# Norms of keys kept compact, g matrices turned and inputs stacked ahead of the kernel taps, scores on four quadrants with masks applied later, and products of constants in TensorE's waits

## The chip, the cores and the metric

One core of one Trainium2 chip runs the whole kernel. The metric is the device time of one execution in microseconds (us), as the median of several runs. Smaller is better.

## What is computed

One decoder layer for 256 tokens of width 1024, all in float32 (gathers and biases in bfloat16 parts). Cut to what matters:

```python
h = rms_norm(x, norm_mix_g)
proj = h @ w_in                                   # 1024 x 2048
y_s5 = s5_mixer(proj[:, :512], ...)               # diagonal complex state space, gelu, glu
y_rw = rwkv7_mixer(h, r, k, v, ...)               # 8 heads of 64
    # kk = k*k_k / |k*k_k| per head; decay; a; g;
    # state = state*w + (state . -kk)(kk*a) + v k;  y = state . r
x = x + concat(y_s5, y_rw) @ w_out
h = rms_norm(x, norm_moe_g)
logits = h @ router_w + router_b                  # top 4 of 32 experts
for e in experts: act = swiglu(h @ w_gate[e] + b, h @ w_up[e] + b); y = act @ w_down[e] + b
x = x + moe;  x = x + sigmoid(rms_norm(x) @ ple_w_gate) * (p @ ple_w_proj);  return rms_norm(x)
```

## The kernel before, in words

All tiles lie in one arena of 47 units of 4 KB per partition (`un(i)`); eight PSUM banks are shared by all stages. Each engine has its program written out by hand, and semaphores (`s[...]`) join them. Three blocks follow one another, with a barrier of all engines between them: the mixers (`layer`, from L276), the router (L1243) and the expert loop (L1379), then a tail (L1549).

**Mixers.** TensorE sums squares (L851 on), then `project(n)` makes 256 columns of the input projection at a time, in `order`, and ScalarE copies each out (`copy_proj`, L395). The low-rank paths follow (`lora_out`, L408, L410). For the S5 mixer VectorE builds products of constants (`products`, L615 to L620), ScalarE pads them into `gpad` (L427) and `opad` (L448), and TensorE makes the `kernel_taps`, turns the 32 `gpad` matrices (`turn_g`, L894; copies at L468), lays out the inputs (`stack_u`; copies at L471) and multiplies (`into`). VectorE takes the phase off (`phase_off`, L635 to L640), scans and puts it back (`phase_on`, L650 to L657). For the RWKV mixer, sums of squares of the keys per head come out as full 128x512 tiles (`head_sums`), with a root on ScalarE (L441) and maximum and reciprocal over 1024 columns on VectorE (L705, L706). The time is cut into 4 chunks of 64; a unit is a chunk of a pair of heads, 16 in all. `pair` issues two 64x64 products, head h on rows and columns h. Five scores of 16 units each come first, masked by VectorE as it copies them from PSUM (L748 to L752). A triangular inverse in 5 levels follows: products `W` (MO by X), a copy by ScalarE (L477), products by Y, an addition by VectorE (L781) and its transpose (L737). In between TensorE turns three arrays (`turn`; copies at L481) and makes the S5 output (`s5_out`; VectorE L661). Then four chunks in turn (ScalarE L486, L492, L496; VectorE L817, L818), with the glu (L501) and parts of the output projection between, and a normalisation (L799 to L811) before the rest of the projection.

GpSimd splits the expert biases into bfloat16 parts (L340 to L344) once their DMAs have landed. SyncE issues the DMAs in a written order, with waits between; a weight slot cannot be filled before the tiles in the same units have been read.

**Router.** Logits, top 4, gates, ranks (VectorE), then the gates are transposed (L1351) and four products of 32 rows with `exp_b_down` start the output accumulation in four banks (L1221).

**Experts.** Each of 32 experts has six chunks of 2 MB (gate 2, up 2, down 2), in a ring of eight slots. Chunks 0, 4 and 5 of expert 0 are issued in the mixers (L304), chunk 1 near their end (L325), chunks 2, 3 and 7 at the start of the router block, chunk 6 at the start of the expert block (L1384), and each later one when TensorE has used the chunk that lies eight before it (L1389). TensorE gathers the tokens (needs the one-hot of L1431), multiplies chunk by chunk, scatters. L1221 and L239 are the `mm` helpers, so most matmuls have one of these lines.

## Time and profile before

| | |
|---|---|
| median of 3 runs | 1209.95 us (1209.51 to 1210.59) |
| profiled execution, its own time | 1203.81 us |
| its span, first to last instruction | 1202.0 us |
| TensorE busy, VectorE, ScalarE, GpSimd | 90%, 30%, 15%, 1% |
| moved by DMA | 430.28 MB, 358 GB/s over the span |
| mean granted TensorE clock | 0.991 |

The busy shares are averages over stages with different limits: the mixers take about the first 220 us, the router 20 us, the experts the rest. A float32 matmul stands in the trace as two records, each with its weight load. Times from the span's start are used below.

### The profile page before, as it was taken

The numbers are of one execution on the slowest core, as the hardware profiler recorded it, in microseconds if no ns is written. First come the engines' busy times: TensorE is split into PE (matmuls) and PEld (weight loads), VectorE is DVE, ScalarE is ACT, GpSimd is POOL, SyncE is SP. The second block draws the span as 40 slices with busy tenths as digits, with TensorE's granted clock in tenths as the row PEclk, the third lists the DMA queues.
The fourth block names the chain that finished last, engine by engine and source line by source line (L and its number), as shares of the span: only waits on it lengthen the run. The fifth ranks groups of instructions, "written<-read, shape, count | busy, mean of one in ns | idle before, by whom it ended". The sixth has DMA issues, their size and how long they took to land. (4 is left out here: it accounts for less than half of the span.)

```text
span 1202.0 us, 18872 instructions
## 1 busy us (share of the span) xinstructions
PE 1076.2 (90%) x8132; PEld 492.5 (41%) x8132; DVE 365.5 (30%) x739; ACT 176.3 (15%) x288; POOL 17.5 (1%) x18
## 2 busy tenths in 40 slices
PE   6989998899999988888888888888888888888896
PEld 5779884443334333333333333333333333333342
DVE  5997925522222111111222111111111221211122
ACT  5580231400000000000000000000000000000023
POOL 0000005000000000000000000000000000000000
PEclk9989999899999999999999999999999999999999
DMA  9301184589999999999999999999999999999970
GB/s 324 125 2 37 43 328 142 211 359 426 428 428 430 428 429 428 427 428 429 429 429 430 428 429 428 428 428 430 429 429 428 429 428 428 427 430 428 430 289 35
DMA packets 44531, 430.28 MB, mean 358 GB/s; under 512 B 4912, under 2 KB 15536, under 8 KB 19920
## 3 DMA queue, kind: packets, MB, share of 16 engines
q1 hardware_dynamic: 44304, 429.24, 85.5%
q8 instruction: 28, 0.46, 0.2%
q0 software_dynamic: 192, 0.52, 0.1%
q14 instruction: 7, 0.06, 0.0%
HBM read 428.70 MB, written 1.05 MB: 358 GB/s over the span
## 5 line engine op out<-in xcount | busy, mean ns | idle before, releaser
L1221 PE MATMUL bank<-arena 128*64 128x512 f32 (+5 forms) x5136 | 847.3, 467 | 91.0 <-DMA arena<-in_exp_w_up 58.3
L1221 PEld LDWEIGHTS bank<-arena 128*64 128x64 f32 (+4 forms) x5136 | 307.8, 128 | 607.0 <-issue 446.2
L239 PE MATMUL bank<-arena 64*64 64x64 f32 (+7 forms) x2048 | 161.6, 264 | 15.4 <-ACT arena L362 8.5
L239 PEld LDWEIGHTS bank<-arena 64*64 64x64 f32 (+3 forms) x2048 | 129.3, 144 | 45.7 <-issue 26.3
L1410 ACT ACTIVATE arena<-arena 128x512 f32<-128x512 f32 x32 | 20.1, 630 | 520.2 <-DVE arena L1458 520.2
L1463 DVE TENSOR_SCALAR arena<-bank 128x512 f32<-128x512 f32 x32 | 22.1, 691 | 227.7 <-PE bank L1221 227.7
L1473 DVE COPY arena<-bank 128x512 f32<-128x512 f32 x32 | 22.1, 691 | 202.8 <-PE bank L1221 202.8
L1458 DVE TENSOR_SCALAR arena<-bank 128x512 f32<-128x512 f32 x32 | 22.1, 691 | 194.0 <-PE bank L1221 194.0
L1413 ACT ACTIVATE arena<-bank 128x256 f32<-128x256 f32 x32 | 12.3, 383 | 326.2 <-PE bank L1517 326.2
L1434 DVE TENSOR_TENSOR arena<-bank,par 128x512 f32<-128x512 f32 x33 | 22.8, 691 | 77.9 <-PE bank L1221 77.9
L1466 DVE SCALAR_TENSOR_TENSOR arena<-arena 128x512 f32<-128x512 f32 x32 | 33.7, 1052 | 1.1
L1461 DVE TENSOR_TENSOR arena<-arena 128x512 f32<-128x512 f32 x32 | 22.1, 692 | 24.5 <-ACT arena L1410 24.5
L1415 ACT ACTIVATE arena<-bank 128x512 f32<-128x512 f32 x32 | 19.1, 597 | 1.7
L1521 PE MATMUL bank<-con,arena 128*128 128x128 f32 x128 | 19.2, 273 | 0.0
L1446 DVE TENSOR_SCALAR arena<-con,arena 128x128 f32<-128x128 f32 x64 | 19.1, 340 | 0.1
L1431 DVE TENSOR_SCALAR arena<-con,arena 128x64 bf16<-128x64 f32 x66 | 13.8, 251 | 14.3 <-PEq L1243 7.5
L1517 PEld LDWEIGHTS bank<-con,arena 128*128 128x128 f32 x64 | 6.5, 141 | 24.3 <-issue 24.3
L1521 PEld LDWEIGHTS bank<-con,arena 128*128 128x128 f32 x128 | 15.0, 140 | 0.0
L239 PE MATMUL bank<-arena,con 128*32 128x64 f32 (+1 forms) x144 | 11.4, 322 | 3.6 <-ACT arena L506 1.4
L1517 PE MATMUL bank<-con,arena 128*128 128x128 f32 x64 | 14.1, 301 | 0.0
L1410 ACT ACT_TABLE_LOAD x8 | 10.3, 1283 | 7.8 <-PEq L1243 7.7
L352 ACT ACTIVATE arena<-par 128x2048 f32<-128x2048 f32 (+1 forms) x7 | 10.3, 1533 | 0.0
(275 smaller groups left out, 406.7 us busy)
## 6 DMA issues: line engine op xcount, KB each, us to landing
arena<-in_exp_w_gate SPq DMA_DIRECT2D x64, 2048.0 KB, 32.2
arena<-in_exp_w_down SPq DMA_DIRECT2D x64, 2048.0 KB, 35.4
arena<-in_exp_w_up SPq DMA_DIRECT2D x64, 2048.0 KB, 35.3
arena<-in_w_in SPq DMA_DIRECT2D x8, 1024.0 KB, 12.9
arena<-in_w_out SPq DMA_DIRECT2D x4, 1024.0 KB, 6.3
...
```

Of the source, the lines that this page charges most:

```text
L239: return nc.tensor.matmul(out, lhsT, rhs, start=start, stop=stop, skip_group_check=True)
L1221: return nc.tensor.matmul(out, lhsT, rhs, start=start, stop=stop, skip_group_check=True)
L1410: nc.scalar.activation(sg, gt, ACT.Sigmoid, scale=1.702).then_inc(s["sig_ready"], 1)
L1415: nc.scalar.activation(actT[:, :, :, :], GATE[:, :].rearrange("p (k h s) -> p k h s", h=2, k=4), ACT.Copy).then_inc(s["actT_ready"], 1)
L1434: tt(xg[:, :, :], GAT[:, :].rearrange("p (k s) -> p k s", k=KD), prm("g_moe_run")[:, :, None].to_broadcast([P, KD, SLOTS]), ALU.mult).then ...
L1458: ts(gt, GATE[:, :], 7.0, None, ALU.min).then_inc(s["gt_ready"], 1)
L1461: tt(sg, sg, gt, ALU.mult).then_inc(s["swish_ready"], 1)
L1463: ts(up, UP[:, :], 7.0, -7.0, ALU.min, ALU.max).then_inc(s["up_read"], 1)
L1466: stt(by_run(gt), plain(up), 1.0, plain(sg), ALU.add, ALU.mult).then_inc(s["act_ready"], 1)
L1473: V.tensor_copy(y, YB[:, :]).then_inc(s["y_ready"], 1)
L1517: last = nc.tensor.transpose(YB[:, t * P:(t + 1) * P], pg[:, t, :], ident)
L1521: last = nc.tensor.transpose(GATE[:, k * P:(k + 1) * P], gt[:, k * P:(k + 1) * P], ident)
```

## The change

- Start: 20 products of ones with ones on TensorE before the squares are summed.
- Keys' norms: the squares are the stationary operand and 2 columns of head sums the moving one, so that 16 numbers per token tile come out; root, maximum and reciprocal run over 128x16; 16 products with the identity spread them again; VectorE multiplies out of PSUM.
- Order: ScalarE pads g after the low-rank outputs, copies the first g matrix of each (`gfirst`) for the taps; `turn_g` is in two halves around `project(4)` and the norms; `stack_u` comes ahead of `kernel_taps`. GpSimd does three memsets that ScalarE (clear of units 2, 3) and VectorE (EL) did.
- Token shift of k and v: ScalarE multiplies by 1 - mu, VectorE adds the shifted rest in 4 instructions instead of 6. ScalarE also scales rk.
- Scores: units 8 to 15 of each score go to the other half of the columns (`cross=True`), interleaved with units 0 to 7; ScalarE copies Mx, RB and RK unmasked, VectorE masks RB and RK in levels 3 and 4. The scans of `phase_on(1)` run ahead of the scores. Head sums of rk move into level 0, `s5_out(3)` into level 4, between its two sets of products. `turn` is in four quadrants too. Chunks 2 and 3 have crossed halves and waits on `first_half`.
- Router: router bias loaded in the mixers; 4 products of constants; gates laid out in four row groups, `exp_b_down` loaded four times, in four DMAs, so that the four bias products use four row groups; 5 products of constants before the first gather. In the expert loop two semaphore waits of VectorE become one.

```diff
+        rbias = bb[:, 0, 0:E]
+        head_pair = head_ones[:, 0:P:CH]
+        norms, rest_mu = u0[:, 0:4 * TT * 2], u0[:, 32:32 + 2 * FT].rearrange("p (m f) -> p m f", f=FT)
...
+                a, o = slice(h * CH, (h + 1) * CH), slice((h ^ cross) * CH, (h ^ cross) * CH + CH)
+                last = mm(out[o], lhsT[a], rhs[a], start, stop)
...
+                sp.dma_start(rbias, io["router_b"].to_broadcast([P, E])).then_inc(p_in, 16)
...
-                sp.dma_start(bias_down, io["exp_b_down"]).then_inc(bias_in, 16)
+                for r in range(4):
+                    hf = r % 2
+                    sp.dma_start(bias_down[r * E:(r + 1) * E, :], io["exp_b_down"][:, hf * 512:(hf + 1) * 512]).then_inc(bias_in, 16)
...
+                pool.wait_ge(s["proj_done"], at_place[0])
+                nc.gpsimd.memset(EL, 1.0).then_inc(s["pool_set"], 1)
+                pool.wait_ge(s["pool_set"], 1)
+                nc.gpsimd.memset(EL[:, :, 0::CH], 0.0).then_inc(s["pool_set"], 1)
+                pool.wait_ge(s["proj_done"], at_place[1])
+                nc.gpsimd.memset(un(2, 2), 0.0).then_inc(s["pool_set"], 1)
...
+                act.wait_ge(s["proj_copied"], at_place[5])
+                rest_of_shift(0, raw["k"], kx, "shift_rest")
...
                 lora_out(0)
...
                 lora_out(1)
                 act.wait_ge(s["kk_ready"], 1)
                 A(kksq[:, :, :], kkn[:, :, :], ACT.Square).then_inc(s["kk_squared"], 1)
+                act.wait_ge(s["pads_clear"], 7)
+                for m in range(2):
+                    act.wait_ge(s["built"], m + 1)
+                    for g in range(2):
+                        a, o = half(g)
+                        A(gpad[m][a, :, :, o].rearrange("p j n c -> p n j c"), gprod[m][a], ACT.Copy).then_inc(s["padded"], 1)
                 copy_proj(2)
                 lora_out(2)
+                act.wait_ge(s["kk_summed"], 1)
+                A(norms, banks[6][:, 0:4 * TT * 2], ACT.Sqrt).then_inc(s["kk_norm"], 1)
+                for m in range(2):
+                    for g in range(2):
+                        a, o = half(g)
+                        A(gfirst[a, m, :, o], gprod[m][a, 0], ACT.Copy).then_inc(s["padded"], 1)
...
-                act.wait_ge(s["kk_summed"], 1)
-                for b in range(2):
-                    m = A(kb[:, 2 * b:2 * b + 2, :], banks[4 + b].rearrange("p (f t) -> p f t", t=T), ACT.Sqrt)
-                m.then_inc(s["kk_root"], 1)
+                for n in range(4):
+                    copy_g(n)
...
-                clear(2, 2)
+                for n in range(4, 8):
+                    copy_g(n)
...
-                A(mag_run[:, :, 1:NK], s5p[:, 15, :][:, :, None].to_broadcast([P, NJ, NK - 1]), ACT.Copy).then_inc(s["mag_ready"], 1)
-                copy_proj(4)
                 copy_proj(5)
-                act.wait_ge(s["pads_clear"], 7)
+                for b in range(2):
+                    act.wait_ge(s["stacked"], b + 1)
+                    A(ustack[:, 8 * b:8 * b + 8, :], banks[2 + b].rearrange("p (j k) -> p j k", k=NK), ACT.Copy).then_inc(s["ustack_ready"], 1)
+                act.wait_ge(s["pool_set"], 3)
                 act.wait_ge(s["taps_done"], 1)
...
+                A(mag_run[:, :, 1:NK], s5p[:, 15, :][:, :, None].to_broadcast([P, NJ, NK - 1]), ACT.Copy).then_inc(s["mag_ready"], 1)
                 copy_proj(6)
+                act.wait_ge(s["scaled"], 3)
+                for i in range(FT):
+                    last = A(rk[:, i, :], rk[:, i, :], ACT.Copy, scale=prm("r_k")[:, i:i + 1])
+                last.then_inc(s["rk_ready"], 1)
                 copy_proj(7)
+                act.wait_ge(s["proj_copied"], 8)
+                rest_of_shift(1, raw["v"], vv, "shift_rest")
+                for m, dst in ((1, Mx), (3, RB), (4, RK)):
+                    for b in range(2):
+                        act.wait_ge(s["scores_done"], 2 * m + b + 1)
+                        A(dst[:, 8 * b:8 * b + 8, :], banks[SCORE_BANK[m] + b].rearrange("p (u t) -> p u t", t=CH), ACT.Copy).then_inc(s["scores_moved"], 1)
...
-                dve.wait_ge(s["proj_done"], at_place[0])
-                link(V.memset(EL, 1.0))
-                link(V.memset(EL[:, :, 0::CH], 0.0))
+                dve.wait_ge(s["pool_set"], 2)
...
+                dve.wait_ge(s["kk_norm"], 1)
+                link(ts(norms, norms, 1e-12, None, ALU.max))
+                V.reciprocal(norms, norms).then_inc(s["kk_norm"], 1)
...
-                dve.wait_ge(s["kk_root"], 1)
-                link(ts(kb, kb, 1e-12, None, ALU.max))
-                link(V.reciprocal(kb, kb))
-                link(tt(kkn, kkn, kb, ALU.mult))
+                dve.wait_ge(s["kk_summed"], 2)
+                for b in range(2):
+                    d = kkn[:, 2 * b:2 * b + 2, :]
+                    last = tt(d, d, banks[6 + b].rearrange("p (f t) -> p f t", t=T), ALU.mult)
+                last.then_inc(s["kk_norm"], 1)
+                dve.wait_ge(s["kk_norm"], 3)
...
+                phase_scan(0)
                 phase_on(0)
                 phase_off(1)
+                phase_scan(1)
...
+                for b in range(2):
+                    dve.wait_ge(s["scores_done"], b + 1)
+                    d = X[:, 8 * b:8 * b + 8, :]
+                    link(tt(d, banks[SCORE_BANK[0] + b].rearrange("p (u t) -> p u t", t=CH), col(C_SU1), ALU.mult))
+                    link(tt(d, d, eye, ALU.add))
+                    turn_x(b).then_inc(s["scores_copied"], 1)
+                for b in range(2):
+                    dve.wait_ge(s["scores_moved"], b + 1)
+                    level_mask(0, b)
+                for b in range(2):
+                    dve.wait_ge(s["scores_done"], 4 + b + 1)
+                    tt(KA[:, 8 * b:8 * b + 8, :], banks[SCORE_BANK[2] + b].rearrange("p (u t) -> p u t", t=CH), col(C_SU), ALU.mult).then_inc(s["scores_copied"], 1)
+
+                phase_on(1)
...
+                    if lev >= LEVELS - 2:
+                        dst = (RB, RK)[lev - LEVELS + 2]
+                        dve.wait_ge(s["scores_moved"], 6)
+                        for b in range(2):
+                            d = dst[:, 8 * b:8 * b + 8, :]
+                            tt(d, d, col(C_UI), ALU.mult).then_inc(s["scores_masked"], 1)
...
+                for _ in range(20):
+                    mm(banks[0][:, 0:P], ones_early, ones_early, True, True)
...
-                head_sums(kksq, 4).then_inc(s["kk_summed"], 1)
+                for n in range(4 * TT):
+                    tok = slice(n // FT * P, (n // FT + 1) * P)
+                    last = mm(banks[6][:, 2 * n:2 * n + 2], kksq[:, n % FT, tok], head_pair, True, True)
+                last.then_inc(s["kk_summed"], 1)
+                turn_g(0)
                 project(4)
+                pe.wait_ge(s["kk_norm"], 2)
+                for n in range(4 * TT):
+                    tile, f = n // FT, n % FT
+                    for h in range(2):
+                        last = mm(banks[6 + f // 2][h * CH:(h + 1) * CH, (f % 2) * T + tile * P:(f % 2) * T + (tile + 1) * P],
+                                  norms[:, 2 * n + h:2 * n + h + 1].to_broadcast([P, CH]), ident, True, True)
+                last.then_inc(s["kk_summed"], 1)
+                turn_g(1)
                 project(5)
+                stack_u()
+                pe.wait_ge(s["kk_norm"], 3)
                 kernel_taps()
-                turn_g()
-                stack_u()
...
+                    bank = SCORE_BANK[m]
+                    for u in range(8):
+                        o = slice(u * CH, (u + 1) * CH)
+                        ins = pair(banks[bank][:, o], fm(l, u), fm(r, u))
+                        if u == 7:
+                            ins.then_inc(s["scores_done"], 1)
+                        last = pair(banks[bank + 1][:, o], fm(l, u + 8), fm(r, u + 8), cross=True)
+                    last.then_inc(s["scores_done"], 1)
...
+                    if lev == 0:
+                        pe.wait_ge(s["rk_ready"], 1)
+                        pe.wait_ge(s["scores_copied"], 4)
+                        head_sums(rk, 0).then_inc(s["rk_summed"], 1)
+                    if lev == LEVELS - 1:
+                        s5_out(FT - 1)
...
-                pe.wait_ge(s["xy_ready"], 2 * LEVELS)
                 pe.wait_ge(s["turned"], 6)
                 pe.wait_ge(s["bonus_ready"], 1)
+                pe.wait_ge(s["scores_masked"], 4)
...
                     if c:
                         pe.wait_ge(s["u0_ready"], c)
                     for i, o in enumerate(tiles):
-                        pair(banks[0][:, o], KA[:, c * FT + i, :], Vs[:, c * FT + i, :], i == 0, False)
+                        last = pair(banks[0][:, o], KA[:, c * FT + i, :], Vs[:, c * FT + i, :], i == 0, False)
+                    if cross:
+                        last.then_inc(s["first_half"], 1)
                     if c:
                         pe.wait_ge(s["y_copied"], c)
                     for i, o in enumerate(tiles):
-                        pair(banks[5][:, o], Vs[:, c * FT + i, :], RK[:, c * FT + i, :], i == 0, False)
+                        last = pair(banks[5][:, o], Vs[:, c * FT + i, :], RK[:, c * FT + i, :], i == 0, False, cross)
+                    if cross:
+                        last.then_inc(s["first_half"], 1)
                     if c:
                         pe.wait_ge(s["state_ready"], c)
+                    if cross:
+                        pe.wait_ge(s["first_half"], 3 * c - 4)
                     for i, o in enumerate(tiles):
-                        last = pair(banks[0][:, o], fm(at, c * FT + i), state[:, o], False, True)
+                        last = pair(banks[0][:, o], fm(at, c * FT + i), state[:, o], False, True, cross)
...
+            for _ in range(4):
+                mm(banks[7][:, 0:P], ident, ident, True, True)
             pe.wait_ge(s["gates_ready"], 1)
-            for tile in range(TT):
-                last = nc.tensor.transpose(banks[5][0:E, tile * P:(tile + 1) * P], gates[:, tile, :], ident)
+            rows = [slice(n * E, (n + 1) * E) for n in range(4)]
+            for n in range(4):
+                last = mm(banks[5][rows[n], 0:P], gates[:, n // 2, :], ident, True, True)
             last.then_inc(s["gates_turned"], 1)
             pe.wait_ge(s["gatesT_ready"], 1)
+            pe.wait_ge(s["ple_copied"], EARLY)
             for n in range(4):
-                if n < EARLY:
-                    pe.wait_ge(s["ple_copied"], n + 1)
-                mm(banks[n][:, :], gatesT[:, n // 2 * P:(n // 2 + 1) * P], bias_down[:, n % 2 * HF:(n % 2 + 1) * HF], True, False)
+                mm(banks[n][:, :], gatesT[rows[n], :], bias_down[rows[n], :], True, False)
...
+            for _ in range(5):
+                mm(YB[:, 0:P], ident, ident, True, True)
```

## Rows read from the trace of the kernel before

**Rows 1.** The page, part 2: GB/s moved in 40 equal slices of the span.

```profile
GB/s 324 125 2 37 43 328 142 211 359 426 428 428 430 428 429 428 427 428 429 429 429 430 428 429 428 428 428 430 429 429 428 429 428 428 427 430 428 430 289 35
```

**Rows 2.** Waits of TensorE, 250 to 1160 us: total us, times, longest.

```profile
PE bank L1221 <- DMA arena<-in_exp_w_up: 58.3, 52, 1.2
```

**Rows 3.** Busy by window: PE, PEld, DVE, ACT, POOL; PEclk; DMA share; GB/s.

```profile
80.00:82.00 2.00, 1.05 (x5) 1.05 (x6) 1.97 (x2) 1.98 (x5) 0.00 (x0) 0.53 0.00 0
...
238.00:240.00 2.00, 1.39 (x2) 0.00 (x0) 0.00 (x0) 0.00 (x0) 0.00 (x0) 0.50 0.62 262
240.00:242.00 2.00, 0.91 (x18) 0.91 (x19) 0.42 (x2) 1.28 (x1) 0.00 (x0) 0.50 0.15 33
...
248.00:250.00 2.00, 2.00 (x12) 0.70 (x10) 0.00 (x0) 0.00 (x0) 0.00 (x0) 1.00 0.41 74
```

**Rows 4.** Timeline at the hand-over: start, us, engine, line; idle before in brackets.

```profile
232.94 6.46 PE L1221 MATMUL bank<-arena 32*128 32x512 f32 x8 [0.46 <-ACT arena L1273]
...
241.09 2.74 PE L1221 MATMUL bank<-arena 128*128 128x64 bf16 x48 [1.70 <-DVE arena L1431]
...
248.62 3.68 SPq L1389 DMA_DIRECT2D arena<-in_exp_w_up  x2
```

**Rows 5.** Timeline of the start, and of project(3) for comparison.

```profile
8.52 5.33 PE L239 MATMUL bank<-arena 128*128 128x256 f32 x16 [8.52 <-ACT arena L362]
...
13.89 0.47 ACT L369 ACTIVATE arena<-bank,par 128x256 f32<-128x256 f32 x1 [1.43 <-PE bank L239]
...
46.95 7.17 PE L239 MATMUL bank<-arena 128*128 128x256 f32 x32
```

**Rows 6.** Timeline of ScalarE and TensorE, 47 to 85 us.

```profile
47.78 4.29 ACT L427 ACTIVATE arena<-arena 64x1024 f32<-64x1024 f32 x4
...
68.70 1.91 ACT L352 ACTIVATE arena<-par 128x2048 f32<-128x2048 f32 x1
...
76.95 1.06 ACT L395 ACTIVATE arena<-bank 128x512 f32<-128x512 f32 x2
...
80.95 3.68 PE L894 MATMUL bank<-con,arena 128*128 128x128 f32 x16 [4.56 <-ACT arena L468]
```

**Rows 7.** Timeline of VectorE, 84 to 111 us.

```profile
84.41 1.20 DVE L667 TENSOR_TENSOR arena<-arena 128x1020 f32<-128x1020 f32 x1
...
92.21 0.69 DVE L635 TENSOR_TENSOR arena<-bank,arena 128x512 f32<-128x512 f32 x1 [2.01 <-PE bank L239]
...
96.12 2.34 DVE L650 TENSOR_TENSOR_SCAN arena<-arena 128x512 f32<-128x512 f32 x2
...
110.74 0.69 DVE L748 TENSOR_TENSOR arena<-bank,con 128x512 f32<-128x512 f32 x1 [4.09 <-PE bank L239]
```

**Rows 8.** Timeline of small products: taps, five scores, one turned array.

```profile
72.46 1.82 PEld L239 LDWEIGHTS bank<-arena 128*32 128x32 f32 x128 [0.33 <-issue]
...
109.54 9.41 PEld L239 LDWEIGHTS bank<-arena 64*64 64x64 f32 x320 [0.33 <-issue]
...
141.21 2.03 PE L239 MATMUL bank<-con,arena 64*64 64x64 f32 x64
```

**Rows 9.** Timeline of the levels and of the first chunk.

```profile
119.84 1.96 PE L239 MATMUL bank<-arena,con 128*128 128x512 f32 x4 [0.75 <-DVE arena L752]
...
121.73 6.74 PE L239 MATMUL bank<-arena 64*64 64x64 f32 x209
...
138.63 0.60 ACT L477 ACTIVATE arena<-bank 128x512 f32<-128x512 f32 x1 [2.85 <-PE bank L239]
...
146.73 0.60 ACT L477 ACTIVATE arena<-bank 128x512 f32<-128x512 f32 x1 [2.84 <-PE bank L239]
...
158.38 1.15 PE L239 MATMUL bank<-arena 64*64 64x64 f32 x32 [0.79 <-DVE arena L781]
```

**Rows 10.** Timeline of VectorE and GpSimd at the normalisation.

```profile
198.81 3.64 DVE L808 TENSOR_SCALAR arena<-arena,par 128x128 f32<-128x128 f32 x4
...
200.83 1.03 POOL L344 CAST arena<-arena 32x1024 bf16<-32x1024 f32 x1
```

207 lines of the change are left out of this document (97 added, 110 removed).

## The prediction, made before the change was run

> **What bounds the kernel now.** I read the DMA rates first, then who waits for whom, then the hand-over from router to experts, then the mixers. From the tenth slice on the DMA moves 425 to 430 GB/s without a break [rows 1]: the expert weights. TensorE waits for them, 52 times for the up chunks alone [rows 2], so the expert loop ends when its stream ends, and a faster TensorE or VectorE in it buys nothing. The stream cannot start early: the slots lie in units that the mixers and the router use. A first load after the barriers goes out late, and the continuous part begins only when TensorE has used chunk 0, at 248.62 [rows 4]. Whatever brings that moment forward moves the end by as much. Around it the DMA is short of full rate: 262, 33 and 74 GB/s against 428 in three windows of 2 us [rows 3], which is 0.8 + 1.85 + 1.65 = 4.3 us of stream, and the windows between are short too. That bounds what the hand-over can give: its gain ends once the queue no longer runs dry, somewhere over 4.3 us. What comes before the router block counts in full.
>
> **Start.** TensorE sums squares in 5.33 us for 16 records of 256 columns; later 32 such records take 7.17, 0.224 each [rows 5]. So 16 would be 3.6 us, and the first few ran at half speed, 1.2 GHz by their duration. The 20 new products (40 records of 128 columns, 0.11 us at full and 0.22 at half speed, half of the 0.224) start at about 1.1 us. Some 3.5 us at half speed, then full, end them near 7.3, ahead of the squares. The sums then end 1.7 us earlier. The root waited 1.43 us for them [rows 5], the rest being its table load, so the gain is 1.4. Bounds: if they stay at half speed to the end they end near 10.1 and delay the sums by 1.6, which gives back all but a little; if the first weights land just then, 0. I take 1.4.
>
> **ScalarE to copy_proj(5).** VectorE cannot shift r before this copy, which ended at 78.0 [rows 6]. ScalarE is busy all the way from 46 us, so I count its work. Out: the clear 1.9; the mag copy 1.1, now behind; the root of 1024 columns 1.1 for one of 16 columns 0.2. In: eight copies of turned g at 0.53 (a 128x512 copy, half of 1.06), 4.3; four copies of gfirst, between 0.2 and 1.07 each (a quarter of the 4.29), the elements being a quarter, so 0.35: 1.4. The root also waits for the norm sums behind `lora_out(2)`; the table load covers most of their 2 us, 1.1 is left. The padding of g only changes its place. With 1.4 from the start: 78.0 - 1.9 - 1.1 - 0.9 + 4.3 + 1.4 + 1.1 - 1.4 = 79.5. The shift of r began at 84.41 [rows 7], since VectorE was held by 1024-column reciprocals and maxima that now vanish; it begins at 79.7.
>
> **VectorE to the scores.** Shift, rk and rt take until 92.21 - 2.01 = 90.2, that is 5.8 us, giving 85.5; the 2.01 us wait for `into` falls away, since TensorE has turned g and stacked u by then: its stall of 4.56 us [rows 6] and the half clock behind it (0.53 granted, 1.2 GHz) [rows 3] go. From 92.21 to 110.74 - 4.09 = 106.65 VectorE works on phases for 14.4 us: 99.9. The second scan with two products, 2.34 + 2 x 0.69 = 3.7, is now before the scores: 103.6. TensorE is ready for them at about 102: 7.5 of its 109.54, the same stall and slow stretch less some 2 us of products that spread the norms, in place of nothing. So VectorE is late next. Masking X begins at 103.6 in place of 110.74.
>
> **Scores.** X takes two times 0.69 + 0.69 + 0.7, till 107.8. TensorE's RB score waits for that (its banks), then ScalarE copies RB, 2 x 0.6, and level 0 starts. On two quadrants 320 records take 9.41 us, 29.4 ns each; the taps, on four column groups, 1.82 us for 128, 14.2 ns each at the same mean of 64 columns [rows 8]. I take four quadrants at that rate: a score 0.95 us in place of 1.9. Level 0 starts at 107.9 + 0.95 + 1.3 = 110.2 in place of 121.73 [rows 9]: 11.5 earlier. The masks of RB and RK, the copy of Mx, the rk scaling (ScalarE, under `project(7)`) leave this chain.
>
> The Trainium skill ("TensorE: Matmul & The Clock Gate", section "Wait — 56ns, not 53.3ns?") says that matmuls never start closer together than about 25 ns. The 14.2 ns of [rows 8] disagree with it. By that rule the scores would gain 0.3 us each and turns 0.3 us, and the sum would come out 3 us higher.
>
> **Levels.** They are bound by TensorE, a level each 146.73 - 138.63 = 8.1 us [rows 9]. Head sums of rk move in, 1.96 [rows 9]. Each of three `turn` falls from 2.03 [rows 8] to 1.0, but behind the third nothing else stands now and the RB mask (2 x 0.65) delays VectorE's addition, so it gives 0.4. `s5_out(3)` only changes place. The first chunk saves 0.79 of waiting for X, yet its glu waits for the gelu as before, so I take 0. Together 1.96 - 1.0 - 1.0 - 0.4 = -0.4: the first chunk starts 11.9 earlier.
>
> **Chunks and normalisation.** Four waits on `first_half` let TensorE drain; never less than 0, at most one record's 0.224 us each: +0.4, about the middle. GpSimd's split starts when the bias DMAs have landed; three more DMAs, and the weights' loads nearer by, make that 1 to 2 us later against the loop. It ran till 201.9, and beside it VectorE took 3.64 us for four 128x128 operations [rows 10]. Two more operations now fall beside it: +0.6 (0 to 1.5). So the router block starts 10.9 earlier. Memsets on GpSimd lie under VectorE's wait before r; uncovered they would cost 1 us.
>
> **Hand-over.** The four bias products take 6.46 us, at half clock [rows 3, 4]. In four row groups they take one's time, 0.9 at full and 1.7 at half clock: -5.5 (-4.7). The barrier follows at once, since the other engines have nothing behind these products. The five products start about when VectorE starts its one-hot, 0.5 us before the gather: 1.1 to 2.2 us of work, +0.6 to +1.7. The gather took 2.74 at 0.50 granted clock [rows 3, 4]; at full clock half: 0 to -1.4. Together -3.0 to -6.3, capped by the idle DMA. I take -5.0, nearer the upper end since 4 products keep TensorE busy ahead of the drop.
>
> **Sum.** 11.9 - 0.4 - 0.6 + 5.0 = 15.9 us. Against the profiled 1203.81 that is 1187.9; the median lies 6.1 above that execution, and so 1194.1. The merged wait in the expert loop is worth 0, under the DMA; uncovered it is some 0.1 us per expert.
>
> **Rivals.**
> *More quadrants bring nothing.* For it: no row shows all four at once with different rows and columns. Against: [rows 8]. Price: 1.0 at RB, 2.4 at the turns, 2.6 at the bias products in series at full clock: 1200.1. Chance 0.10.
> *The clock falls among the scores.* TensorE idles from about 104.8 to 107.9 for X. It fell to 0.53 behind the 4.56 us stall [rows 3, 6]; this gap is shorter. Some 3 us of work at half speed would be added: 1197.1. Chance 0.20. The Trainium skill ("TensorE: Matmul & The Clock Gate", section "What's actually happening") calls the half clock the default to which an idle TensorE returns; with that the trace agrees.
> *ScalarE or the norms are later.* ScalarE's chain has no slack left, and a late item (turned g, norms, u) stops TensorE and then VectorE. At 4 us: 1198.1. Chance 0.16.
> *Slower.* The clock falls as above and the levels do not lift it: the 32-row products ran at half clock till they ended without lifting it [rows 3, 4], and the levels' tiles are of 64. Price: the 36 us from level 0 to the chunks, doubled: 1230. It decides once more than 16 us of TensorE-bound work runs at half clock. Head sums on all rows speak against it. Chance 0.04.
> *Nothing arrives.* The stream would be held by something not tied to the mixers: 1210. [rows 2, 4] speak against. Chance 0.05.
>
> **Numbers.** The forecast has 0.45: 1194.1. Upward, quadrants, clock and late ScalarE reach 1200 together with a flat start and a hand-over at -3; downward the hand-over's full 6.3 and no cost at the normalisation give 1191.8, and some ends I can't see. I take 1189.5 to 1202. A measurement of this kernel tells 0.2% (2.4 us) from no change. Faster 0.91, same 0.05, slower 0.04.
>
> **What would show it.** Root near 12.5; the r shift near 80; X near 103.6; level 0 near 110; first chunk near 146.5; bias products in 1 to 2 us; first refill about 16 us before 248.6, and the tail as far ahead. Wrong: a granted clock of 0.5 between 105 and 180, scores at 29 ns per record, or a router block that starts over 14 or under 7 us earlier.

## The result, and the profile after

The changed kernel takes 1200.73 us, the median of 9 runs (1198.24 to 1209.95); the kernel before, beside it on the same chip, takes 1209.51, the median of 9 (1204.73 to 1210.59). The ratio is 0.9947, with a 95% interval from 0.9924 to 0.997. So it is faster, by about 6.4 us. The forecast of 1194.1 was 6.6 us too low, though the time lies in the range. The runs of each kernel scatter about as widely as the two differ (5.9 us those of the kernel before, 11.7 those of the changed one), which will matter below.

The two profiled executions differ by less: 1200.06 against 1203.81 us, span 1198.3 against 1202.0. They are what the sum was made on: it said -15.9, and -3.7 came. That the median missed by only 6.6 is luck: the forecast put it 6.1 above the profiled execution, as in the kernel before, and it lies 0.7 above.

The timeline of the changed kernel (start, us, engine, line; idle before and its releaser in brackets), from several stretches, of all five engines:

```profile
12.49 0.47 ACT L383 ACTIVATE arena<-bank,par 128x256 f32<-128x256 f32 x1
16.36 29.93 PE L243 MATMUL bank<-arena 128*128 128x256 f32 x144 [4.19 <-DMA arena<-in_w_in]
48.14 7.17 PE L243 MATMUL bank<-arena 128*128 128x256 f32 x32
...
106.74 0.69 DVE L803 TENSOR_TENSOR arena<-bank,con 128x512 f32<-128x512 f32 x1 [0.39 <-PE bank L243]
111.10 0.33 PE L243 MATMUL bank<-arena 64*64 64x64 f32 x4 [2.60 <-DVE arena L798]
112.36 5.60 PE L243 MATMUL bank<-arena 64*64 64x64 f32 x188 [0.93 <-issue]
127.20 2.37 PE L243 MATMUL bank<-arena 64*64 64x64 f32 x74 [1.29 <-issue]
...
186.46 1.04 POOL L354 CAST arena<-arena 128x1024 bf16<-128x1024 f32 x1 [129.28 <-DMA arena<-in_exp_b_down]
194.70 6.45 DVE L865 TENSOR_SCALAR arena<-arena,par 128x128 f32<-128x128 f32 x4
203.49 13.06 PE L243 MATMUL bank<-arena 128*128 128x512 f32 x24 [4.76 <-DVE arena L868]
...
223.78 0.82 SPq L1344 DMA_DIRECT2D arena<-in_exp_w_up  x2
234.97 1.14 PE L1315 MATMUL bank<-arena 32*128 32x512 f32 x8 [0.40 <-ACT arena L1368]
238.55 1.56 PE L1315 MATMUL bank<-arena 128*128 128x64 bf16 x48
244.90 3.68 SPq L1486 DMA_DIRECT2D arena<-in_exp_w_up  x2
```

And the windows of the changed kernel, with the columns of [rows 3]: busy PE, PEld, DVE, ACT, POOL; granted clock; DMA share; GB/s.

```profile
16.00:18.00 2.00, 1.65 (x6) 1.46 (x7) 2.00 (x6) 2.00 (x2) 0.00 (x0) 0.85 1.11 353
18.00:20.00 2.00, 2.00 (x6) 1.55 (x6) 1.97 (x2) 1.98 (x3) 0.00 (x0) 0.50 1.05 380
...
106.00:108.00 2.00, 2.00 (x152) 2.00 (x148) 1.58 (x3) 1.97 (x6) 0.00 (x0) 1.00 0.57 147
...
112.00:114.00 2.00, 1.64 (x81) 1.64 (x84) 2.00 (x5) 0.29 (x1) 0.00 (x0) 0.74 0.03 8
114.00:116.00 2.00, 1.88 (x65) 1.70 (x60) 1.91 (x3) 1.38 (x4) 0.00 (x0) 0.50 0.00 0
...
202.00:204.00 2.00, 0.51 (x1) 0.50 (x2) 1.97 (x3) 0.00 (x0) 0.16 (x1) 0.50 0.00 0
...
238.00:240.00 2.00, 2.00 (x55) 1.98 (x53) 0.15 (x1) 0.58 (x1) 0.00 (x0) 1.00 0.94 401
```

The kernel before at the same places (its matmuls are L239): the first projections, the gap in its levels, GpSimd's split, the output products, and the router block's first load.

```profile
16.88 28.21 PE L239 MATMUL bank<-arena 128*128 128x256 f32 x144 [3.03 <-DVE arena L556]
129.56 3.71 PE L239 MATMUL bank<-arena 64*64 64x64 f32 x119 [1.09 <-issue]
186.18 1.04 POOL L340 CAST arena<-arena 128x1024 bf16<-128x1024 f32 x1 [182.65 <-DMA arena<-in_exp_b_down]
203.96 10.57 PE L239 MATMUL bank<-arena 128*128 128x512 f32 x24 [1.16 <-DVE arena L811]
222.15 0.90 SPq L1249 DMA_DIRECT2D arena<-in_exp_w_up  x2
```

Read from top to bottom. The root starts at 12.49 as forecast, but TensorE then waits 4.19 us for the first weights, its clock falls to half, and project(3) starts at 48.14, later than before [rows 5]. X is masked at 106.74, 4.0 us earlier than in [rows 7]; behind the scores TensorE waits 2.60 us for those masks, then 0.93 for nothing that the profile shows, and the clock is at half again. In the levels it stands still again, 1.29 us and then 0.60. The first chunk starts at 154.26, 4.1 earlier than [rows 9]. All of that is lost at the normalisation: four 128x128 operations take 6.45 us, TensorE waits 4.76 for them, its clock falls, and the router block's first load goes out at 223.78, 1.6 us later than before (222.15). The hand-over (from the router block's first load to the first refill, the load that starts the unbroken stream) then gives 5.35: from that load to the first refill 21.1 us in place of 26.5, with the bias products in 1.14 us and the gather in 1.56 at full clock, where [rows 4] have 6.46 and 2.74. The refill at 244.90 is 3.7 earlier than [rows 4], as the end is.

So there are four places to explain: the front, the scores and levels, the normalisation, and the hand-over that came out right.

### The profile page after: what moved, and what is told of

The parts are those of the page before. It is cut to its first block and busy times, and to the rows that moved or that the text cites. A ratio compares the mean times of both kernels' runs of the same rounds, so it can differ in the third digit from the quotient of the medians.

```text
span 1198.3 us, 19087 instructions
## 1 busy us (share of the span) xinstructions
PE 1076.2 (90%) x8240; PEld 494.3 (41%) x8240; DVE 357.3 (30%) x730; ACT 183.5 (15%) x309; POOL 20.4 (2%) x21
## 5 line engine op out<-in xcount | busy, mean ns | idle before, releaser
L243 PE MATMUL bank<-arena 64*64 64x64 f32 (+8 forms) x2088 | 169.7, 272 | 16.8 <-DVE arena L868 4.8
L243 PEld LDWEIGHTS bank<-arena 64*64 64x64 f32 (+3 forms) x2088 | 134.7, 152 | 48.5 <-issue 25.2
L1512 ACT ACTIVATE arena<-bank 128x512 f32<-128x512 f32 x32 | 19.1, 598 | 1.7
L243 PE MATMUL bank<-arena,con 128*32 128x64 f32 (+1 forms) x140 | 8.4, 255 | 1.9 <-ACT arena L547 1.4
L409 ACT ACTIVATE arena<-bank 128x512 f32<-128x512 f32 x8 | 5.8, 721 | 25.0 <-PE bank L243 25.0
```

The source lines that it names most:

```text
L243: return nc.tensor.matmul(out, lhsT, rhs, start=start, stop=stop, skip_group_check=True)
L1512: nc.scalar.activation(actT[:, :, :, :], GATE[:, :].rearrange("p (k h s) -> p k h s", h=2, k=4), ACT.Copy).then_inc(s["actT_ready"], 1)
```

## The experiments

The kernel before ran beside each set on the same chip. Times below are those of the profiled execution (span) unless a median is named. The experiments are called e1 to e17, after the labels of their expectations; those at the front (e1, e6), e3, e4, e9, e10 and e11 are single runs.

### The front

The first test takes the 20 warm-up products out, the second keeps them and puts 12 more behind the sums of squares.

```diff
-                for _ in range(20):
-                    mm(banks[0][:, 0:P], ones_early, ones_early, True, True)
```

> The changed kernel without the 20 products ahead of the sums of squares; all else as changed. Theory W: the products gain nothing, because project(0) waits for its weights (16.36 us in the changed kernel, 16.88 before), and they lengthen TensorE's idle stretch ahead of it from 3.0 to 4.2 us, in which the granted clock falls to 0.50. Without them project(0) starts at 16.9, its records take 0.22 us each, no window from 16 to 24 shows a clock under 1, project(3) starts at 46.9 to 47.2 instead of 48.14, the shift of r (VectorE) at 80.7 to 81.0 instead of 81.98, and the first chunk 1.1 us earlier. Rival: the slow stretch has another cause (DMA, ScalarE's clear of the ninth unit); then project(3) stays at 48.1 or comes later, by the 0.5 us of the later start.

```diff
                 last.then_inc(s["rms_summed"], 1)
+                for _ in range(12):
+                    mm(banks[0][:, 0:P], ones_early, ones_early, True, True)
```

> The changed kernel with 12 more of the warm-up products, behind the sums of squares, where TensorE waits 4.19 us for the first weights. Nothing is left out. Theory (the early sums only lengthen the wait for the weights, and behind it the clock falls to half for 4 us of project(0)): project(0) still starts at 16.4 to 16.7, since the weights land then, but runs at full clock and takes 28.2 us in place of 29.93, project(3) starts at 46.4 to 46.8 in place of 48.14, the shift of r 1 to 1.7 us before 81.98, and the end comes 1 to 2 us before 1198.3. Rival (the load of the weights is what is slower, 13.6 against 12.9 us): project(0) takes 29.5 to 30 again, and nothing moves by more than 0.4.

TensorE's timeline without the warm-up products:

```profile
8.46 5.65 PE L243 MATMUL bank<-arena 128*128 128x256 f32 x16 [8.46 <-ACT arena L376]
17.14 28.21 PE L243 MATMUL bank<-arena 128*128 128x256 f32 x144 [3.03 <-DVE arena L601]
47.21 7.17 PE L243 MATMUL bank<-arena 128*128 128x256 f32 x32
```

TensorE's timeline with 12 more of them, and two windows of that kernel below it:

```profile
16.59 7.61 PE L243 MATMUL bank<-arena 128*128 128x256 f32 x34 [1.55 <-DMA arena<-in_w_in]
...
46.69 7.17 PE L243 MATMUL bank<-arena 128*128 128x256 f32 x32
```

```profile
16.00:18.00 2.00, 1.41 (x7) 1.26 (x8) 2.00 (x6) 2.00 (x2) 0.00 (x0) 1.00 1.11 351
18.00:20.00 2.00, 2.00 (x11) 1.77 (x10) 1.97 (x2) 1.98 (x3) 0.00 (x0) 1.00 1.05 380
```

Without the products (e1) the first weights are used 0.8 us later (17.14 against 16.36), and project(3) still starts 0.9 us earlier, because the first projections take 28.21 us in place of 29.93. With the bridge (e6) the clock stays at 1.00, project(3) starts at 46.69 and the shift of r at 80.53, 1.45 us before the changed kernel; the end came at 1196.1. The load isn't slower, as the rival had it: the weights land at 16.3 to 16.6 in every kernel with the warm-up. So the warm-up does what was forecast for the sums (3.72 us for the 16 records where it is read alone), and the time it saves is waited away in front of the weights, long enough for the clock to fall. Behind waits of 4.02 to 4.24 us it fell in all 12 traces that have the warm-up and no bridge, behind 1.55 and 1.56 in the two with the bridge it stayed up. A wait of 3.03 us decides nothing by itself: the clock stayed up behind it in the kernel before, in e1 and in e16, and fell in e8, which also leaves out the warm-up (further down):

```profile
18.20 29.62 PE L243 MATMUL bank<-arena 128*128 128x256 f32 x144 [3.03 <-DVE arena L601]
```

```profile
18.00:20.00 2.00, 1.80 (x4) 1.51 (x5) 2.00 (x7) 2.00 (x2) 0.00 (x0) 0.50 1.06 380
```

There project(3) starts at 49.67, later than in the changed kernel. So to leave the warm-up out is no sure cure; to fill the wait was one in both traces that have it.

### The normalisation

First the split of the biases was held back until VectorE's normalisation is over, then its loads were moved ahead of those of w_out and the slots, so that the split is done before it.

```diff
                 pool.wait_ge(s["bonus_ready"], 1)
+                pool.wait_ge(s["mix_rw_ready"], 2)
...
-                        act.wait_ge(s["bias_split"], 10)
+                        act.wait_ge(s["bias_split"], 5)
```

> The changed kernel with GpSimd's split of the expert biases held back until both token tiles are normalised (it then runs beside the last output products); ScalarE's wait before it overwrites the first bias tile asks for the 5 steps that read that tile, and no more for all 10. Theory G: in the changed kernel the split falls beside VectorE's first normalisation, because the chunks end 4 us earlier while the bias DMAs land no earlier; both slow down (four 128x128 operations in 6.45 us, 3.64 before, 1.11 alone), TensorE then waits 4.76 us and its clock falls to 0.50 for some 6 us. Held back, the four operations take 1.1 us, TensorE's wait before the output products is under 1 us, its clock stays at 1, and the router block starts 7 to 9 us earlier, at 215 to 217 instead of 223.8; some of it is given back where the split meets VectorE's residual. The end comes 5 to 9 us earlier. Rival: VectorE's slowness has another cause than GpSimd; then the router block stays at 223 to 224.

Its VectorE, first at the normalisation, then at the residual:

```profile
194.45 1.12 DVE L866 TENSOR_SCALAR arena<-arena,par 128x128 f32<-128x128 f32 x4
...
208.19 3.23 DVE L896 TENSOR_SCALAR arena<-arena,small 128x1024 f32<-128x1024 f32 x1
```

```diff
-                sp.wait_ge(s["s5_out_done"], 4)
-                for c in (1, 2):
-                    sp.dma_start(wout[c][:, :, :], wo[c]).then_inc(wout_in, 16)
...
                 sp.wait_ge(s["scaled"], 4)
                 sp.wait_ge(s["phase_on"], 2)
...
+                sp.wait_ge(s["s5_out_done"], 4)
+                for c in (1, 2):
+                    sp.dma_start(wout[c][:, :, :], wo[c]).then_inc(wout_in, 16)
...
```

> The changed kernel, but the loads of the expert biases are issued before the loads of wout and the slots (their own waits kept), and the load of wproj behind them. Nothing is left out. GpSimd's split, which now runs from 186.5 to 202.2 beside VectorE's normalisation, should then run beside the chunk loop and be done before the last y copy. Theory N (the normalisation lost about 5 us because the split still ran beside it, so that four 128x128 operations take 6.45 us in place of 1.1 and TensorE's clock falls): the row of four operations falls to 1.1 to 1.5, TensorE's wait of 4.76 us is gone, the router block's first load goes out 3 to 5 us before 223.8, and the span falls by 3 to 4.5, so about 1194 to 1195.5 against 1198.3. Rival M (contention only moves, as it did when the split was held back): the chunk loop's VectorE operations are slowed, the last y copy comes 3 us or more later than 187.7 and the router block starts within 1 us of 223.8.

(The lines left out take the loads of the slots, pT, the router's bias and wproj along, behind those of the expert biases.) Its GpSimd, VectorE and TensorE:

```profile
147.42 1.04 POOL L354 CAST arena<-arena 128x1024 bf16<-128x1024 f32 x1 [90.03 <-ACT arena L522]
...
162.44 1.11 POOL L358 CAST arena<-arena 32x1024 bf16<-32x1024 f32 x1
...
191.10 17.33 PE L243 MATMUL bank<-arena 128*128 128x512 f32 x40
193.73 1.11 DVE L865 TENSOR_SCALAR arena<-arena,par 128x128 f32<-128x128 f32 x4
```

Held back (e2), the split lets the four operations run in 1.12 us, but meets the next ones: a 128x1024 scaling takes 3.23 us where it takes 1.26 in the changed kernel, and the router block's load goes out at 223.22, 0.6 us earlier. There is a second cost that I had overlooked: the barrier ahead of the router block waits for every engine, GpSimd too, and its split now ends at 222.4; TensorE stood idle for 8.1 us before 223.26, with its clock at half from 216.6. The contention was only moved (median 1202.37, ratio to before 0.9962, interval 0.9946 to 0.9979). Done early (e5), beside the chunk loop, it costs nothing there: the last y copy is at 187.13 (187.72 in the changed kernel), TensorE goes through its 40 records without a wait, and the load goes out at 215.65, 8.1 us earlier. The span is 1191.2, 7.1 less than the changed kernel's; I had expected 3 to 4.5. The profiled execution, 1192.96, is the fastest of 4; the others took 1195.04 to 1199.72. The median is 1196.97, the ratio to before 0.9906 (0.9886 to 0.9927), so by the ratios (0.9906 against 0.9947) the move is worth some 5 us.

The Trainium skill ("SBUF — State Buffer", section "SBUF: two separate sides") has VectorE and GpSimd share one pair of ports as an exclusive lock, held for a whole instruction, but for VectorE only where its operation runs in a mode with two ports or has two inputs in SBUF. The traces agree in form: the four operations took 1.6 us each beside GpSimd operations of 1.03 to 2.13 us and 0.28 alone, while the reciprocal, with one input, took 3.35 in both.

### The scores

Three tests (e3, e4, e7): the pairs back on two quadrants; 12 constant products in the gap before RB; and RB and RK in banks 2 and 3, so that the gap has no cause.

```diff
         def pair(out, lhsT, rhs, start=True, stop=True, cross=False):
+            cross = False
```

> The changed kernel with every crossed product put back on the straight halves (scores, turned arrays, chunks 2 and 3), so that only two quadrants of the array are used; order and everything else as changed. Theory Q: four quadrants give about 0.9 us per score and 0.7 us per turned array, but the first scores lie in a stretch in which VectorE is late, so that only the scores behind the masked X and the three turned arrays count. Level 0 starts 0.5 to 1.5 us later, each turned array takes 2.03 us instead of 1.33, and the first chunk starts 2 to 3.5 us later than 154.26. If TensorE's idle stretch ahead of the fourth score shrinks enough for the clock to stay at 1, 1 to 2 us of this come back. Rival: the four quadrants bring nothing; then the turned arrays take the same 1.3 us and the first chunk starts at 154 to 154.5.

Its windows behind the first three scores:

```profile
112.00:114.00 2.00, 1.60 (x50) 1.58 (x51) 2.00 (x5) 0.00 (x0) 0.00 (x0) 1.00 0.04 8
114.00:116.00 2.00, 2.00 (x76) 2.00 (x74) 1.97 (x5) 1.09 (x2) 0.00 (x0) 1.00 0.00 0
```

With two quadrants TensorE is busy for longer and waits only 0.63 us for X; its clock stays at 1.00 through scores and levels. In the changed kernel it runs 65 small records in the same window at half clock, here 76 at full. That is why the quadrants bought only 0.6 us at the first chunk (156.15 against 155.56 for its first copy) and 0.95 at the last y copy: 2 to 3.5 had been expected. Nor are these 0.6 earned in this stretch: the first score already starts 0.48 later than in the changed kernel (105.96 against 105.48).

```diff
                     if m == 3:
+                        for _ in range(12):
+                            mm(banks[2][:, 0:P], ident, ident, True, True)
                         pe.wait_ge(s["scores_copied"], 2)
```

> The changed kernel with 12 products of the identity with itself (a bank that nothing uses then) in TensorE's wait ahead of the fourth score. Theory C: TensorE stands idle for 2.6 us there after short work, the clock is granted at 0.50 to 0.74 from 112 to 116 us, and the fourth score, the fifth and the first products of level 0 run at half speed. With the 12 products (12 x 0.11 to 0.22 x 2 records, some 2.7 us) no window from 110 to 118 is under 1, the copies of RB end 1 us earlier than 114.8, level 0's first copy by ScalarE starts at 115 to 116 instead of 117.07, and the first chunk 1 to 2 us earlier than 154.26. Rival: the gap between the fourth score's first records and the rest (0.93 us, nothing seen to release it) is what costs, and it stays; then the gain is under 0.7 us.

```diff
-        SCORE_BANK = (4, 6, 0, 4, 6)
+        SCORE_BANK = (4, 6, 0, 2, 2)
...
-                    if m == 3:
-                        pe.wait_ge(s["scores_copied"], 2)
...
```

> The changed kernel, but the scores RB and RK go to banks 2 and 3 instead of 4 to 7, so that RB no longer waits for the masks of X, and level 0 no longer for the copy of RB. Nothing is left out. Theory C (the first three scores, in half the time, left TensorE idle for 2.6 us, its clock fell to half, and RB, RK and level 0 took back at half speed what the quadrants had gained): with that wait gone the granted clock stays at 1.00 from 104 to 125, RB is over by 110, RK by 112, the first W copy starts at 113 to 114 in place of 117.07, the first addition to X at 117 to 118 in place of 121.0, and the first chunk starts 3 to 3.7 us before 154.26. End: 2.5 to 3.7 us less than 1198.3. Rival V (VectorE with its masks and phases is the bound behind the scores): the W copy comes earlier, but the first addition to X no more than 1 us, and the end by under 1 us. Rival F (TensorE waits for its own instructions): gaps without a releaser of over 2 us appear between 105 and 125 and the W copy moves by under 2 us.

The edit moves other waits with the banks: RK waits for both copies of RB, level 0 for VectorE's masks of X, and `s5_out(0)` for the copies of RK.

TensorE's timeline with the 12 products:

```profile
112.54 3.89 PE L243 MATMUL bank<-con 128*128 128x128 f32 x19 [3.05 <-issue]
```

TensorE's timeline with the other banks:

```profile
113.91 1.15 PE L243 MATMUL bank<-arena 64*64 64x64 f32 x59 [3.75 <-issue]
116.24 5.38 PE L243 MATMUL bank<-arena 64*64 64x64 f32 x128 [1.18 <-ACT arena L514]
```

Both miss, and in the same way. The work that should have filled the gap didn't start: TensorE stood still for 3.05 and 3.75 us with every semaphore that it needs set, and then ran at half clock. In the second the first W copy came 2.9 us later than in the changed kernel (119.95), and the end at 1200.5 (median 1203.56; ratio to before 0.9972, 0.9952 to 0.9992); the first ended at 1198.3, as the changed kernel did. Of the 2.9 us, 1.55 came from ahead of the scores: the first began at 107.03 in place of 105.48, since the clock fell at 60.4 already, behind the small norm products of 128x2. It fell there, between 57.8 and 62.0, in six of the 17 traces (e7, e8, e11, e13, e16, e17), which no run explains. What was missing behind the scores were instructions. The DMA view of that stretch lists, beside 1 MB of w_out, the queue that brings them, three packets of 16 KB:

```profile
q1 hardware_dynamic: 272, 1.05, 18.7%
q8 instruction: 3, 0.05, 1.0%
```

The traces bear this out. In all 17 of this family the gaps without a releaser between taps and levels stand at the same places in the count of TensorE's matmul records from the start of the execution (600, 980 or 981, 1107, 1360, 1486, and so on, at distances that are multiples of some 127; no trace has all of them). They do so although the scores begin at record 784, in the kernels without warm-up at 744 and in those with the bridge at 808, so that 170 to 240 records of the stage are through when the first gap comes (in e11, where it is the next one, 323). And each ends 1.2 to 1.6 us after a packet of 16 KB of that queue is through: in the changed kernel the packet of 110.12 took 0.95 us, and TensorE goes on at 112.36; in e7 it is 111.60, 0.96 and 113.91. The gap lasts until the next packet has come.

That gave two theories, which the next pair tells apart by moving two w_out loads to the place of the other two.

```diff
-                sp.dma_start(wout[3][:, :, :], wo[3]).then_inc(wout_in, 16)
...
-                for c in (1, 2):
+                for c in (3, 0, 1, 2):
```

> The changed kernel with two of the four loads of w_out (1 MB each; they now go out at 105.6 and 120.3) moved behind the last s5_out product, at about 151, where the other two are. Nothing is left out. In the changed kernel TensorE stands still without a releaser for 0.93 us behind the first and 1.29 us behind the second of these loads. Theory B (its instructions are fetched by the same DMA engines, and wait behind the megabyte): both gaps shrink to under 0.4 us, and the first W copy comes 0.5 to 1 us, the second level's 1.5 to 2 us earlier; the end by 1 to 2 us. Rival A (a run of some 250 small products at 13 to 15 ns each simply outruns the fetch, as at 82 where a gap of 1 us stands with no other transfer near it): both gaps stay within 0.3 us, and the end within 0.5 us of 1198.3.

> RB and RK in banks 2 and 3, as before, and the two w_out loads moved behind the last s5_out product. Nothing is left out. With the banks alone TensorE stood still for 3.75 us without a releaser, from 110.2 to 113.9, while 1 MB came in from 107.1 on, and its clock fell to half. Theory B: without the load the gap is under 1.2 us, the granted clock stays at 1.00 up to 120, the first W copy starts at 113.5 to 115.5 in place of 119.95, and the end falls to 1195 to 1197 from 1200.5. Rival A: the gap stays at 2.5 us or more, the clock falls, and the end is at 1199.5 to 1201.

TensorE's timeline of the first:

```profile
85.41 25.17 PE L243 MATMUL bank<-arena 128*32 128x96 f32 x376 [1.58 <-issue]
...
116.92 1.97 PE L243 MATMUL bank<-arena 64*64 64x64 f32 x61 [0.95 <-issue]
...
120.73 8.26 PE L243 MATMUL bank<-arena 64*64 64x64 f32 x262
```

TensorE's timeline of the second:

```profile
111.47 1.15 PE L243 MATMUL bank<-arena 64*64 64x64 f32 x59 [1.57 <-issue]
```

Each theory holds for a part. The gap in the levels is gone (262 records without a break), that of 3.75 us has become 1.57. With the load right behind the first score the packet that ends the gap starts 2.9 to 4.7 us after that score (11 traces), without it 1.3 to 2.6 (six traces): a megabyte in flight does hold the instructions up. But 0.95 us stay behind the scores, and 1.58 behind the taps, at 83.8, where no load runs: 170 to 330 records at 13 to 15 ns each outrun the fetch alone. How the gaps in the levels come about isn't settled. e4 ran its 262 records there without a break too, although a load of w_out had gone out at 123.22, and e12, without these loads, has a gap of 0.84 us in a turned array. The levels became 2.5 us shorter in e11 (its first W copy is 0.9 later, but 1.15 earlier counted from its first score, which starts at 107.56; its first chunk copy is 1.6 earlier), the end only 0.8, since the normalisation's wait grew to 6.2 us. The second (e12) still lost its clock behind the scores and ended at 1198.7 (median 1199.46, ratio 0.9937, 0.9914 to 0.996).

The Trainium skill ("Runtime: NRT & Kernel Launch", section "Instruction fetch mechanics") has instructions come in blocks of 16 KiB, at a cost "mostly hidden". The block size agrees with the packets; hidden it isn't here.

### All together, and what the quadrants are worth

> Both edits together (biases loaded early; RB and RK in banks 2 and 3), and the 20 warm-up products at the start left out, which alone gave 1.8 us. Nothing that reaches an output is left out. If the three costs are independent, as my account has them, they add: 1.8 + 3 + 3.5 = 8.3 us less than the changed kernel, a span near 1190, 14 us below the kernel before, ratio near 0.988. If one of the two new edits only moves its cost, 4 to 5 us less. If everything is hidden by something later, under 2.

> The biases loaded early, RB and RK in banks 2 and 3, and the w_out loads late; the warm-up products kept. Nothing is left out. The early biases alone gave a span of 1191.2. If theory B holds for the pair above, this one gives 1187.5 to 1189.5; if rival A does, the banks cost 2 us here too and it gives 1192.5 to 1194. Against the kernel before a ratio of 0.988 to 0.990, or 0.992 to 0.994.

> The best kernel so far (biases early, RB and RK in banks 2 and 3, w_out late; span 1190.3) with the scores and turns back on two quadrants. Nothing is left out. There the granted clock stayed at 1.00 from 82 to 122. If the quadrants are worth what I forecast where the clock holds, RB, RK and the third turn each lose 0.95 us on the path: the first W copy comes 0.5 to 1 us after 116.36 (VectorE's masks of X end at about 112.8 and cover the rest), the first chunk 2.5 to 3.5 us later, the end 2 to 3.5 later. Rival (a run of small products at half the rate no longer outruns TensorE's instructions, so the gaps without a releaser, 3.0 us in four places, shrink to under 1.5 and give most of it back): the first chunk 0 to 1.2 us later, and the end within 1.2 us of 1190.3.

> The best kernel without the 20 warm-up products. Nothing that reaches an output is left out. If the front is where they cost, the shift of r comes 0.9 us earlier, the first chunk 0.9 to 1.8 and the end 1 to 2 us before 1190.3. If the gain of e1 was an accident of where the instruction blocks fall, the front still gives 0.9, but a gap without a releaser moves elsewhere (as it did with both edits, where the clock fell for the whole of project(6)), and the end is anywhere from 1189 to 1198.

> The best kernel with the 12 further products behind the sums of squares. Nothing is left out. By the clock theory for the front, project(0) runs at full clock, everything up to the scores comes 1.3 to 1.7 us earlier, and the end at 1188.5 to 1189.3. By the rival, 1190 to 1191.

| kernel | median, us (runs) | ratio to before, 95% | each run: us at mean granted clock |
|---|---|---|---|
| e8: early biases, banks, no warm-up | 1203.37 (6) | 0.9937 (0.9912 to 0.9962) | 1194.65 at 0.993; 1202.26 at 0.990; four of 1202.98 to 1204.19 at 0.986 or 0.987 |
| e13: early biases, banks, late w_out | 1191.94 (6) | 0.988 (0.9858 to 0.9901) | 1190.66 to 1192.93 at 0.993; 1194.56 at 0.990 |
| e15: e13 on two quadrants | 1194.76 (5) | 0.9882 (0.9866 to 0.9899) | 1193.33 to 1196.46 at 0.992 to 0.995; 1203.31 at 0.987 |
| e16: e13 without warm-up | 1197.12 (4) | 0.9889 (0.9851 to 0.9928) | 1192.68 and 1192.93 at 0.994; 1201.31 at 0.989; 1201.51 at 0.986 |
| e17: e13 with 12 more products | 1189.53 (4) | 0.9835 (0.9818 to 0.9851) | 1188.13 to 1190.36 at 0.994 to 0.996; 1193.12 at 0.993 |

The first missed by far: 8.3 us had been expected, and the fastest run of six (span 1192.9) shows 5.4. The timeline of its profiled run and one of its windows say what the others paid:

```profile
87.44 12.94 PE L243 MATMUL bank<-arena 128*32 128x32 f32 x80 [1.27 <-issue]
```

```profile
90.00:92.00 2.00, 2.00 (x11) 2.00 (x11) 0.77 (x2) 1.43 (x2) 0.00 (x0) 0.50 0.00 0
```

The gap behind the taps, 1.27 us, stands in all kernels of this family (1.0 to 1.7 us); 14 of the 17 traces keep their clock through it, and where it falls, the stretch from into(0) into project(6) runs at half clock, and X is masked at 116.78 in place of 106.74 (1.5 of these 10 us come from the front). Behind the scores this kernel then waited 3.07 us for instructions. In the profiled runs of e15 and e16 the same fall is seen. So these kernels can lose 8 to 9 us by a small accident, and medians of a few runs count accidents; what the two-quadrant kernel (e15) tells must be read from its undisturbed runs: 1193.33 to 1196.46 against 1190.66 to 1194.56, medians 1194.75 and 1191.94. Taken as they stand the quadrants would be worth 2.8 us, within the forecast (2 to 3.5). But the two ran on different chips, where the kernel before had medians of 1209.17 and 1205.75, and the ratios to it, 0.9882 and 0.988, show no difference. The only trace of e15 is of its disturbed run; it has no gap without a releaser in scores and levels, only the one behind the taps, where e13 has four in all, 3.0 us. Whether the quadrants pay is open.

The kernel without warm-up (e16) gave neither the front's 0.9 in its median nor a loss in every run: two runs of four fell. The one with the bridge (e17) holds its clock best and is the fastest of all, 0.9835 of the kernel before, some 20 us. It beats both kernels.

### The hand-over

> The changed kernel with its four bias products all in row group 0, one behind the other, in place of four row groups: the expert biases of the second half and the gates of the second tile are computed from the wrong rows, so that the output's bias part is another one. Theory: the four groups are worth three products, so the products take 3.4 to 4 us in place of 1.14 at the full clock the 4 constant products keep, and the first refill comes 2.3 to 2.9 us later after the router block's first load than 21.1 us; the end moves by as much, since the DMA is idle there. Rival: the bank count, not the row groups, is what counts, and they take 1.1 to 1.5 in series as well.

> The changed kernel without the 4 and the 5 constant products at the hand-over. Nothing that reaches an output is left out. Theory (they hold the clock that the four bias products and the gather need): the bias products take 1.7 to 2.2 us in place of 1.14, the gather 2.4 to 2.8 in place of 1.56, the granted clock falls to 0.5 behind the gates' wait, and the first refill comes 1 to 2 us later after the router block's first load than 21.1 us. Rival (the work after the drop is so short that the clock doesn't matter, and the five products delay the gather): the refill comes 0.3 to 1 us earlier after that load, and the end with it.

The first kernel (e9) takes all four bias products from row group 0 (`gatesT[rows[0], :], bias_down[rows[0], :]`), so that its output is another one; the second (e10) has neither the 4 nor the 5 constant products. TensorE's timeline of the first:

```profile
235.70 3.70 PE L1315 MATMUL bank<-arena 32*128 32x512 f32 x8 [0.40 <-ACT arena L1368]
240.62 2.50 PE L1315 MATMUL bank<-con 128*128 128x128 f32 x10 [1.23 <-PEq L1339]
242.91 2.77 PE L1315 MATMUL bank<-arena 128*128 128x64 bf16 x48
```

TensorE's timeline of the second, and one window of it:

```profile
235.54 1.14 PE L1315 MATMUL bank<-arena 32*128 32x512 f32 x8 [0.40 <-ACT arena L1368]
238.77 2.74 PE L1315 MATMUL bank<-arena 128*128 128x64 bf16 x48 [2.09 <-DVE arena L1526]
```

```profile
238.00:240.00 2.00, 1.23 (x24) 1.23 (x25) 0.42 (x2) 1.15 (x1) 0.00 (x0) 0.50 0.97 418
```

The row groups are worth 3.70 - 1.14 = 2.56 us of products; behind them in series the clock falls as well, and from the router block's load to the first refill it takes 27.8 us in place of 21.1. Without the constant products the bias products keep their 1.14 us, so these don't need the four ahead; the gather falls to half clock (2.74 for 1.56), as does the first half of chunk 0, and the refill comes 24.15 us after the load: 3.05 us, and 3.5 at the end, where I had expected 1 to 2. Both sets were taken out at once, so which of them is worth the 3.05 isn't shown.

## Why the prediction was right or wrong

The step that failed most is the normalisation, put at +0.6 us and measured at +5.7; the front, the scores and the levels failed by some 2.5 us each. By the prediction's own steps, each as change of a milestone:

| step | forecast | measured | off by |
|---|---|---|---|
| front, project(3) | -1.4 | +1.2 | +2.6 |
| from there to the masks of X | -5.7 | -5.2 | +0.5 |
| masks of X to level 0 | -4.4 | -1.85 | +2.55 |
| levels to the first chunk | -0.4 | +1.7 | +2.1 |
| chunks | +0.4 | 0 | -0.4 |
| normalisation | +0.6 | +5.7 | +5.1 |
| hand-over | -5.0 | -5.35 | -0.35 |
| sum | -15.9 | -3.8 (the end: -3.7) | +12.1 |

**Front: wrong.** The step "the gain is 1.4" followed the gain to the root and not to the next thing that TensorE needs. The first weights land at 16.4; before, TensorE used them at 16.88. At most 0.5 us could arrive, and the longer wait cost 1.7 in clock. The prediction named this, "if the first weights land just then, 0", and took the other end; a loss had no place among its bounds.

**ScalarE, VectorE: right.** The chain to copy_proj(5), counted operation by operation, was off by 0.3 once the front is taken out (the shift of r at 81.98 in place of 79.7). The rival that ScalarE or the norms are late did not come.

**Scores: the rival of the clock came,** at 0.20 the likeliest of the rivals, and was sized well (3 us, 2.55 measured). Of the 2.55, 0.93 are the gap without a releaser, and the rest lies in the stretch at half clock: the size is in part luck, and the cause was only half seen. Faster scores lengthen the wait for X, which I had said; that they also outrun the instructions I had not. The rate itself was right: 152 records in a window of 2 us is 13 ns each, on all four quadrants, against the 29.4 of [rows 8]. It also disagrees with the 25 ns of the Trainium skill ("TensorE: Matmul & The Clock Gate", section "Wait — 56ns, not 53.3ns?"), as the taps' 14.2 did.

**Levels: wrong by 2.1,** of which 1.17 are gaps without a releaser: three, 1.29 + 0.60 + 0.37 = 2.26, in place of one of 1.09. Some 0.8 are the turned arrays, which took 1.4 us each where I had 1.0. The gap of 1.29 was gone without the loads of w_out (e11), but also in e4, which has them; the other two stand 5 and 20 us behind the landing of the load, and the cause stays open.

**Normalisation: the largest miss.** The step "that makes it 1 to 2 us later against the loop ... two more operations now fall beside it: +0.6 (0 to 1.5)" had the mechanism and missed the size. The split began at 186.46, as late as before (it ended at 201.9 then, at 202.2 now): it didn't move with the loop at all, since the landing of the bias loads, its releaser in the row above, sets it. So the path slid 4.1 us against it, and the split now covered all four operations and the ones around them, 6.45 + 1.53 + 1.07 us for 1.11 + 0.69 + 0.69. TensorE waited 4.76 us for that, and its 24 records then took 13.06 us, at half clock for the first 5 us, where before they took 10.57 behind a wait of 1.16, and at full clock take 10.4 (24/40 of the 17.33 of e5). A gain upstream was turned into a collision downstream. Everything that had been won before the last y copy was lost here; with the biases early the same kernel is 7.1 us faster in the profiled executions and some 5 by the ratios.

**Hand-over: right,** and for the reason given; the cap by the idle DMA did not bind below 5.35.

**The other rivals.** That quadrants bring nothing, and that nothing arrives, are refuted. The slow case, a clock low through the levels, did not happen there, but its kin does: in some executions it stays low from the taps into project(6), for 8 to 9 us. Of the prediction's own signs of being wrong two came: a granted clock of 0.5 between 105 and 180, and a router block less than 7 us earlier, for it came 1.6 later. The scores at 29 ns a record did not.

The profiled execution of the kernel before, taken as the base of the sum, ran at a mean clock of 0.991; most of its runs take 1205 to 1210.6 at 0.984 to 0.990. The medians differ by 8.8 where the profiles differ by 3.7. No trace shows where the kernel before loses its clock in those runs, so whether the change cures a part of it stays open.
